# Attention heads pipelined over shared interludes, index heads scored in pairs

## What is computed

```python
# first block: DSA, 8 heads, keys picked by 16 index heads
logits = einsum('thd,sd->ths', qi, k_idx) * idx_scale        # 16 heads of 64
score = einsum('th,ths->ts', wi * w_scale, relu(logits))     # summed over heads
_, sel = top_k(where(causal, score, -inf), 64)
q_lat = einsum('shd,hdc->shc', q, w_uk)                      # query to latent, 256
s = einsum('thc,tkc->thk', ql, c_sel) * HEAD_DIM ** -0.5 - slopes * dist
o_lat = einsum('thk,tkc->thc', softmax(s), c_sel); o = einsum('shc,hcd->shd', o_lat, w_uv)
# first block: MoBA, 8 heads; 256 tokens are one block, so this is causal attention
p = softmax(q @ k.T * scale - slopes * dist, causal); o = p @ v
merged = sigmoid(ga + b0) * (o_a @ w_o_dsa) + sigmoid(gb + b1) * (o_b @ w_o_moba)
# second block: three branches of 4 heads, each with a gate of 2048 columns:
# forgetting attention, banded attention with relative bias, stick-breaking attention
```

## Time and profile before

| what | value |
|---|---|
| median of three timed runs | 2283.29 us (2281.11 to 2289.33) |
| the profiled execution | 2280.53 us |
| its span | 2278.7 us |
| granted TensorE clock, mean over the span | 0.993 |
| TensorE busy | 2240.7 us (98%) |
| VectorE, ScalarE, GpSimd busy | 57%, 46%, 7% |

### The profile page before, as it was taken

How to read it: one execution, slowest core, us unless ns; L and a number is a source line. 1 busy time by engine, 2 the same in 40 slices (tenths; PEclk the granted TensorE clock), 3 DMA queues, 4 the chain that set the end, 5 groups by cost and what they waited for, 6 DMA issues and landing times.

```text
span 2278.7 us, 29566 instructions
## 1 busy us (share of the span) xinstructions
PE 2240.7 (98%) x10185; PEld 1849.8 (81%) x10185; DVE 1307.2 (57%) x1571; ACT 1039.1 (46%) x1239; POOL 169.6 (7%) x175
## 2 busy tenths in 40 slices
PE   8999999999999899999999999998999999999999
PEld 7877888888877678888888888886888888888887
DVE  5545655666657655455444544557656566645674
ACT  4343544555434444443444344434455444545642
POOL 1000000001204040000000000004000000200020
...
GB/s 218 231 160 159 174 157 154 194 175 211 256 180 165 150 184 185 184 196 191 194 187 191 192 180 201 184 195 143 171 174 202 200 192 174 210 183 175 174 186 165
DMA packets 216435, 421.24 MB, mean 185 GB/s; under 512 B 15224, under 2 KB 19360, under 8 KB 214432
## 3 DMA queue, kind: packets, MB, share of 16 engines
...
...
## 4 chain that ended last, share of the span: by engine, by line
PE 95%; DVE 3%; DMA 1%; ACT 1%; issue 0%; ACTq 0%; DVEq 0%; SPq 0%
PE b_ps L549 89%; PE b_ps L574 1%; PE b_ps L591 1%; PE b_ps L634 1%; DVE b_x_res L1547 1%; DMA b_stage<-in_w_out 1%; PE b_ps L707 1%; DVE b_x_res L1538 1%; DVE b_w_lo L1387 1%; PE b_ps L649 1%; DMA b_stage<-in_w_in 0%; PE b_ps L643 0%; PE b_ps L730 0%; PE b_ps L650 0%; DVE b_x_res L1526 0%
## 5 line engine op out<-in xcount | busy, mean ns | idle before, releaser
L1387 DVE TENSOR_TENSOR b_w_lo<-b_stage,b_w_hi 128x1024 fp32r<-128x1024 f32 (+1 forms) x762 | 934.2, 1245 | 621.4 <-ACT b_w_hi L1000 617.5
L1000 ACT ACTIVATE b_w_hi<-b_stage 128x1024 fp32r<-128x1024 f32 (+1 forms) x762 | 794.6, 1054 | 698.0 <-PE b_ps L549 658.7
L549 PE MATMUL b_ps<-b_w_hi,b_x_hi 128*128 128x512 f32 (+1 forms) x2368 | 943.3, 398 | 4.9 <-DVE b_x_lo L1428 4.3
L549 PE MATMUL b_ps<-b_w_hi,b_x_lo 128*128 128x512 f32 (+1 forms) x2368 | 924.2, 390 | 0.0
L549 PE MATMUL b_ps<-b_w_lo,b_x_hi 128*128 128x512 f32 (+1 forms) x2368 | 923.2, 390 | 0.0
L549 PEld LDWEIGHTS b_ps<-b_w_hi,b_x_hi 128*128 128x128 f32 x2368 | 447.2, 189 | 100.4 <-issue 5.2
L549 PEld LDWEIGHTS b_ps<-b_w_hi,b_x_lo 128*128 128x128 f32 x2368 | 446.8, 189 | 94.3
L549 PEld LDWEIGHTS b_ps<-b_w_lo,b_x_hi 128*128 128x128 f32 x2368 | 447.5, 189 | 88.2
L549 PE MATMUL b_ps<-b_w_hi,b_ff_h 128*128 128x512 f32 x352 | 137.2, 390 | 0.0
L549 PE MATMUL b_ps<-b_w_hi,b_ff_l 128*128 128x512 f32 x352 | 137.0, 389 | 0.0
L549 PE MATMUL b_ps<-b_w_lo,b_ff_h 128*128 128x512 f32 x352 | 137.0, 389 | 0.0
...
## 6 DMA issues: line engine op xcount, KB each, us to landing
...
```

Source lines behind the costliest of these rows:

```text
L549: ins = mm(ps[:, ACC + r, 0:n], x[:, kt + t, rows], w[:, slot, t, 0:n], start=first and t == 0 and k == 0, stop=last and t == GK - 1 and k ...
L1000: act.activation(w_hi[:, slot, :, 0:n], stage[:, slot, :, 0:n], ACT.Copy)\
L1387: dve.tensor_tensor(w_lo[:, slot, :, 0:n], stage[:, slot, :, 0:n], w_hi[:, slot, :, 0:n].bitcast(F32), ALU.subtract).then_inc(sem("lo_done ...
```

## The change

In the five attention stages the hooks count groups over all four blocks, g = 8 i + j, 0 to 31, and the hardware loops over blocks are written out. Every `STEP` = 3 groups (DSA, MoBA) or `STEP_2` = 5 groups (branches) there is one interlude k, and it holds pieces of different heads. In DSA: outputs of head k - 3, turn of k - 2, scores of k - 1, query of k. In MoBA and the branches: outputs of k - 2, turn (or the sums of the third branch) of k - 1, scores of k. VectorE has `logits_in` and the remainder of an output at that group, `normalise` one group later, and the halving of the bias another group later. The call of `gates_in` stays at j = 7 of each block, behind what falls on this group. GpSimd stages queries and values in the matching order, and in DSA issues the load of `w_uk` ahead of the copy of values. Index heads are scored two at a time after groups 0 and 4, the second into the bank `OT` and through `aux_b`.

```diff
+STEP = 3
+STEP_2 = 5
...
-            with c.loop(pool, "dsa", H_DSA - 1) as i:
-                stage_values(i)
-                pool.wait_ge(sem("x_done"), i + 2)
-                load(w_uk_st[:, :], a["w_uk"][ds((i + 1) * HD, HD), :], "uk")
-            stage_values(H_DSA - 1)
+            for k in range(H_DSA + 2):
+                if k + 1 < H_DSA:
+                    pool.wait_ge(sem("x_done"), k + 2)
+                    load(w_uk_st[:, :], a["w_uk"][(k + 1) * HD:(k + 2) * HD, :], "uk")
+                if k >= 2:
+                    stage_values(k - 2)
...
+                stage_q(0)
+                stage_v(0)
+                for k in range(n + 1):
+                    if k >= 2:
+                        stage_v(k - 1)
+                    if k + 1 < n:
+                        stage_q(k + 1)
...
                     pe.wait_ge(sem("qi_staged"), c.next("qi_staged"))
                 pe.wait_ge(sem("idx_read"), c.value("idx_read"))
-                for t, (lo, hi) in enumerate(TILE_COLS):
-                    ins = mm(ps[:, AUX, lo:hi], qi_st[half, n // 2, t * P:(t + 1) * P],
-                             kidx_t[half, 0:hi - lo], start=True, stop=True)
-                ins.then_inc(sem("idx_done"), 1)
-                c.next("idx_read")
+                for n, bank in enumerate((AUX, OT)):
+                    half = slice(n * IDX_D, (n + 1) * IDX_D)
+                    for t, (lo, hi) in enumerate(TILE_COLS):
+                        ins = mm(ps[:, bank, lo:hi], qi_st[half, j // 4, t * P:(t + 1) * P],
+                                 kidx_t[half, 0:hi - lo], start=True, stop=True)
+                    ins.then_inc(sem("idx_done"), 1)
+                    c.next("idx_read")
...
-                def dsa(j):
-                    if j == 0:
-                        query_latent(i * 2)
-                    elif j == 1:
-                        lat_scores()
-                    elif j == 2:
-                        query_latent(i * 2 + 1)
-                    elif j == 3:
-                        turn_probs()
-                    elif j == 4:
-                        outputs()
-                        lat_scores()
-                    elif j == 6:
-                        turn_probs()
-                    elif j == 7:
-                        outputs()
-                weights(hook=dsa)
...
+            def dsa(g):
+                if g % STEP:
+                    return
+                k = g // STEP
+                if 0 <= k - 3 < H_DSA:
+                    outputs()
+                if 0 <= k - 2 < H_DSA:
+                    turn_probs()
+                if 0 <= k - 1 < H_DSA:
+                    lat_scores()
+                if k < H_DSA:
+                    query_latent(k)
+            for i in range(4):
+                weights(hook=lambda j: dsa(i * 8 + j))
...
+            def moba(g):
+                if g % STEP:
+                    return
+                k = g // STEP
+                if 0 <= k - 2 < H_MOBA:
+                    outputs()
+                if 0 <= k - 1 < H_MOBA:
+                    turn_probs()
+                if k < H_MOBA:
+                    head_scores(k, km_t)
+            for i in range(4):
+                weights(hook=lambda j: moba(i * 8 + j))
...
+                def branch(g):
+                    if g % STEP_2:
+                        return
+                    k = g // STEP_2
+                    if 0 <= k - 2 < H_B2:
+                        outputs()
+                    if 0 <= k - 1 < H_B2:
+                        if n < 2:
                             turn_probs()
+                        else:
+                            stick_sums()
+                    if k < H_B2:
+                        if n < 2:
+                            head_scores(k, k2_t)
+                        else:
+                            stick_scores(k)
+                for i in range(4):
+                    weights(hook=lambda j: branch(i * 8 + j))
...
+            def dsa(g):
+                if g % STEP:
+                    return
+                k = g // STEP
+                if 0 <= k - 3 < H_DSA:
+                    out_hi(flat(oh[:, k - 3:k - 2, :]))
+                if 0 <= k - 2 < H_DSA:
+                    probs_out("o_done")
+                if 0 <= k - 1 < H_DSA:
+                    c.next("s_done")
+                if k < H_DSA:
+                    aux_out(aux_a, "s_done")
+                if 0 <= k - 1 < H_DSA:
+                    exps()
...
+                for n, relu in enumerate((relu_s, aux_b)):
+                    h = b * 4 + j // 2 + n
+                    dve.wait_ge(sem("idx_read"), c.next("idx_read"))
+                    for t, (lo, hi) in enumerate(TILE_COLS):
+                        ins = dve.scalar_tensor_tensor(
+                            out=score[:, lo:hi], in0=relu[:, lo:hi],
+                            scalar=flat(w_idx[:, t:t + 1, h:h + 1]),
+                            in1=score[:, lo:hi], op0=ALU.mult, op1=ALU.add)
+                    ins.then_inc(sem("relu_used"), 1)
...
-                def dsa(j):
-                    if j == 0:
-                        dve.tensor_scalar(bias_d[:, :], bias_d[:, :], 0.5, None, ALU.mult).then_inc(sem("dve_step"), 1)
-                        dve.wait_ge(sem("dve_step"), c.next("dve_step"))
-                    if j == 4:
-                        out_lo(flat(oh[:, ds(i * 2, 1), :]), flat(ol[:, ds(i * 2, 1), :]))
-                    if j in (1, 4):
-                        softmax(bias_d[:, :])
-                    if j in (3, 6):
+            def halve(bias):
+                dve.tensor_scalar(bias[:, :], bias[:, :], 0.5, None, ALU.mult).then_inc(sem("dve_step"), 1)
+                dve.wait_ge(sem("dve_step"), c.next("dve_step"))
+            def dsa(g):
+                k = g // STEP
+                if g % STEP == 0:
+                    if 0 <= k - 2 < H_DSA:
                         c.next("t_done")
-                    if j == 3:
-                        dve.tensor_scalar(bias_d[:, :], bias_d[:, :], 0.5, None, ALU.mult).then_inc(sem("dve_step"), 1)
-                        dve.wait_ge(sem("dve_step"), c.next("dve_step"))
+                    if 0 <= k - 1 < H_DSA:
+                        logits_in(bias_d[:, :])
+                    if 0 <= k - 3 < H_DSA:
+                        out_lo(flat(oh[:, k - 3:k - 2, :]), flat(ol[:, k - 3:k - 2, :]))
+                elif g % STEP == 1:
+                    if 0 <= k - 1 < H_DSA:
+                        normalise(TILE_COLS, logits[:, 0, :])
+                elif k < H_DSA:
+                    halve(bias_d)
+            for i in range(4):
+                def in_block(j):
+                    dsa(i * 8 + j)
                     if j == 7:
                         gates_in(gate_a, vec_a, i)
-                        out_lo(flat(oh[:, ds(i * 2 + 1, 1), :]), flat(ol[:, ds(i * 2 + 1, 1), :]))
-                weights(hook=dsa)
+                weights(hook=in_block)
...
+            def moba(g):
+                k = g // STEP
+                if g % STEP == 0:
+                    if 0 <= k - 1 < H_MOBA:
                         c.next("t_done")
-                    if j == 6:
-                        out_lo(flat(oh[:, ds(i * 2 + 1, 1), :]), flat(ol[:, ds(i * 2 + 1, 1), :]))
+                    if k < H_MOBA:
+                        logits_in(bias_m[:, :])
+                    if 0 <= k - 2 < H_MOBA:
+                        out_lo(flat(oh[:, k - 2:k - 1, :]), flat(ol[:, k - 2:k - 1, :]))
+                elif g % STEP == 1:
+                    if k < H_MOBA:
+                        normalise(TILE_COLS, logits[:, 0, :])
+                elif k + 1 < H_MOBA:
+                    halve(bias_m)
+            halve(bias_m)
+            for i in range(4):
+                def in_block(j):
+                    moba(i * 8 + j)
                     if j == 7:
                         gates_in(gate_b, vec_b, i)
-                weights(hook=moba)
+                weights(hook=in_block)
...
+                def branch(g):
+                    k = g // STEP_2
+                    if g % STEP_2 == 0:
+                        if 0 <= k - 2 < H_B2:
+                            y_in(k - 2)
+                        if 0 <= k - 1 < H_B2:
+                            if n < 2:
+                                c.next("t_done")
+                            else:
+                                stick_out()
+                        if k < H_B2:
+                            if n < 2:
+                                logits_in(flat(bias4[:, k:k + 1, :]), ALU.subtract if n == 0 else ALU.add)
+                            else:
+                                stick_in()
+                    elif g % STEP_2 == 1:
+                        if 0 <= k - 2 < H_B2:
+                            y_lower(k - 2)
+                        if k < H_B2:
+                            if n < 2:
+                                normalise(TILE_COLS, logits[:, 0, :])
+                            else:
```

(5 more changed lines are left out.)

331 lines of the change are left out of this document (136 added, 195 removed).

## The result

The changed kernel takes 2292.66 us (median of 15 runs, 2289.47 to 2295.78), the kernel before 2281.66 us (15 runs, 2280.47 to 2289.33). The ratio is 1.0043, 95% interval 1.0036 to 1.005: slower, by 11.0 us. The forecast was 2303 and a range from 2294. It also lies inside the 0.5% that the prediction names as the least it can tell from no change; the interval of the ratio excludes 1 all the same.

The account below looks back on a forecast made before the run. TensorE was taken as the bound: 22.0 us of stalls at block ends less 1.5 saved by merges and index pairs gave +20.5 on the median of 2283.3, said as 2303 us, range 2294 to 2313.

Parts of the forecast that it names:

- The bound: Whole kernel: TensorE, busy 98% of the span, is the bound; whatever makes it wait is added to the time.
- the price of an interlude: Small matmuls between two weight groups: full interlude costs the sum of its parts, 1.64 us in MoBA, 3.16 in DSA.
- Stalls at block ends: Attention stages: VectorE's gate copy waits behind queued score work, twelve TensorE stalls, 22.0 us, between 17 and 27.
- branch 2's first: Third branch, group 7: TensorE waits 3.45 us for VectorE's gate copy, behind a late weight part and four term operations.
- MoBA's second: MoBA, group 15, both interlude and block end: TensorE ready at 1.64, copy done at 4.7, a 3.0 us stall.
- Merged interludes: DSA, MoBA and branches: 45 fewer interludes save 0 to 1.4 us, 0.5 taken.
- The index pairs: Index heads scored two at a time: 8 pairs save about 1.0 us, between 0 and 4.6.
- the 0.29 over: Index head of 64 rows: 0.95 us against a 0.66 us score; the 0.29 excess is what a pair could share.
- Its sign to look for: Profile after, index stage: a pair of index heads must cost a little under 2 x 0.95 us.
- The half-way rival: Stalls as forecast, index pairs fully overlapped by the skill's rule: 2303 - 6.6 = 2296 to 2297 us; chance 0.07.
- The clock: Rival: clock falls in the longest stalls, two to four falls, 3 to 9 us more, 2306 to 2312; chance 0.2.
- Slower by more than 0.5%: Whole kernel: chance 0.86 of slower, meaning above 2294.7 us; same 0.12, faster 0.02.

Follow-up runs that it names:

- no_stall: Changed kernel with gates' read first in DSA, MoBA and third branch, STEP_2 = (4, 4, 5), third branch's terms two groups after scores: 2273.38 us, ratio 0.9964.

## Why the prediction was wrong, and where it was right

**The bound, and the price of an interlude: right.** TensorE stayed at 98%. In the kernel after, MoBA's full interlude costs 1.64 us, as in the sum, DSA's 3.17 against 3.16.

**Stalls at block ends: right.** All twelve came at the named groups, for 20.7 us instead of 22.0. The longest is branch 2's first, then MoBA's second, as named. DSA's group 23 missed by the most, 0.38 for 0.7; the other eleven came out within 0.25 us each. The queue of an engine that runs in order can be added up row by row from the trace of before.

**Merged interludes: inside the range, near its upper end.** 0.5 was taken, between 0 and 1.4; the ledger of the kernel after leaves 1.2. In `no_stall`, DSA, MoBA and the first two branches, which have one stall left (0.84 at MoBA's group 23), give 1.2 for 39 merges: 0.03 each, the very hundredths that the prediction counted as rounding.

**The index pairs: this step failed.** The prediction took half of "the 0.29 over", 1.0 us for 8 pairs, and set the upper end at 4.6. It is 8.5 us, 1.07 for each pair. Two things were wrong in it. First, the size of what sharing an interlude saves: the 0.29 was the excess over a 128-row score, and half of it was taken, where the run with pairs of the same half shows 0.43. That is 8 x 0.43 = 3.4 us, within the ends given. Second, the other 0.63 for each pair, 5.1 us, is the second head running beside the first, and the sum had no term for it. Its sign to look for, a pair a little under 2 x 0.95, came out at 1.20 - 0.23 = 0.97. The error of 10.3 us is made of 7.5 here, 1.3 in the stalls, 0.7 in the merges, and 1.6 in the starting point (the median of three runs, 2283.29, where fifteen give 2281.66), less 0.8 by which 2303 was rounded down.

The overlap stood in the prediction, as a rival with a chance of 0.07. Eight matmuls of two row halves in 1.20 us and of one half in 1.84 (138.84 to 140.68) show that matmuls in different halves overlap. The Trainium skill, "TensorE: Matmul & The Clock Gate", Part 3, says this of a weight load whose row group differs, and also that several small matmuls run at the same time in different tiles of the array. The runs agree: the whole second head is hidden. The prediction drew on the first statement only. The half-way rival gave 2296 to 2297; less 0.9 (8.5 for 7.6), 1.3 (the stalls), 0.7 (the merges) and 1.6 (the starting point) it is about 2292, the time that was measured. All that the prediction sets against it is "No row of before has two such heads in a row". That is no evidence against it: a silent trace leaves the matter open, so the rival deserved much more than 0.07, and the range an end below 2294.

**The clock: right as a rival, not in the measured profile.** With waits of up to 3.29 us the kernel after kept 1.00 in the stretches shown. Other kernels of this study fell behind waits of 1.87, 2.57, 2.83, 2.84, 3.28 and 3.29 us, at 1.5 to 1.6 us a fall where it could be set against the same place without one. Two to four falls are then 3 to 6 us, the lower part of the prediction's 3 to 9. The fall is not decided by the length of the wait alone. The prediction set its waits of 3.0 and 3.45 us between one of 2.07 that kept the clock and one of 4.27 that did not; the trace of before has another wait of 2.07, at 675.93, behind which the clock fell.

**Slower by more than 0.5%: the chances missed.** 0.86 stood on slower, which the prediction set at above 2294.7; 2292.66 is 0.48% above 2281.66.
